# First modulation of a transformer kernel in eight pieces, and its first projection multiplied one feature tile at a time

## The reference

```python
c_act = jax.nn.silu(c)                               # (1, 1024)
mod = c_act @ ada_w[layer] + ada_b[layer]            # (1, 6 * 1024)
sh1, sc1, g1, sh2, sc2, g2 = jnp.split(mod, 6, -1)
hmix = rmsnorm(x, norm_mix[layer]) * (1.0 + sc1) + sh1
proj = hmix @ w_in                                   # hgrn2_mixer: q, f, v, g, 1024 columns each
q, f_pre, i_in, g = jnp.split(proj, 4, -1)
log_f = jnp.log(lb + (1.0 - lb) * jax.nn.sigmoid(f_pre))
k = (1.0 - lb) * jax.nn.sigmoid(-f_pre)
```

## Time and profile before

| | |
|---|---|
| median of 3 runs | 2296.42 us (2296.18 to 2296.62) |
| profiled execution, first to last instruction (span) | 2294.8 us |
| around the span (median less span; the page gives no other time of the profiled execution) | 1.6 us |
| PE busy | 98% of the span, granted clock 0.998 |
| DVE, ACT, POOL busy | 72%, 46%, 28% |
| first matmul of a projection | 39.7 us after the span's start |

### The profile page before, as it was taken

How to read it: one execution, slowest core, us unless ns; L and a number is a source line. 1 busy time by engine, 2 the same in 40 slices (tenths; PEclk the granted TensorE clock), 3 DMA queues, 4 the chain that set the end, 5 groups by cost and what they waited for, 6 DMA issues and landing times.

```text
span 2294.8 us, 34769 instructions
## 1 busy us (share of the span) xinstructions
PE 2247.6 (98%) x14151; PEld 1950.4 (85%) x14151; DVE 1641.8 (72%) x2121; ACT 1051.0 (46%) x1515; POOL 634.8 (28%) x559
## 2 busy tenths in 40 slices
PE   7999999999999999999999999999999999999999
PEld 5888778999887877778999888999887868899987
DVE  6668557889785456637888657989456984788844
ACT  4322534555334457734555346444345363544432
POOL 0110223332122048803332011332011870233200
PEclk9999999999999999999999999999999999999999
DMA  8654156775763210026774526775333202787322
GB/s 333 191 166 140 46 174 165 185 180 122 267 211 102 82 57 1 1 65 168 190 185 119 162 95 173 175 185 120 101 97 98 81 30 76 191 191 173 105 92 83
DMA packets 224373, 308.69 MB, mean 135 GB/s; under 512 B 14345, under 2 KB 165446, under 8 KB 223958
## 3 DMA queue, kind: packets, MB, share of 16 engines
q1 hardware_dynamic: 173268, 223.99, 30.1%
q0 software_dynamic: 50640, 82.29, 17.4%
q10 hardware_dynamic: 306, 0.19, 0.0%
HBM read 302.23 MB, written 4.19 MB: 134 GB/s over the span
## 4 chain that ended last, share of the span: by engine, by line
PE 85%; DVE 9%; POOL 2%; ACT 2%; issue 1%; DMA 1%; ACTq 0%; DVEq 0%
PE ps L733 42%; PE ps L1181 10%; PE ps L1183 10%; PE ps L1182 10%; PE ps L880 4%; DVE w_lo L2320 2%; DVE dsa_mask L3127 1%; PE ps L1307 1%; POOL nsa_p L3498 1%; PE ps L1323 1%; DVE small L3125 1%; PE ps L929 1%; ACT w_hi L1635 1%; DMA m_raw<-in_ada_w 1%; DVE h_lo L2417 1%
## 5 line engine op out<-in xcount | busy, mean ns | idle before, releaser
L2320 DVE TENSOR_TENSOR w_lo<-w_raw,w_hi 128x1024 fp32r<-128x1024 f32 (+1 forms) x466 | 652.5, 1401 | 478.7 <-ACT w_hi L1635 477.0
L1635 ACT ACTIVATE w_hi<-w_raw 128x1024 fp32r<-128x1024 f32 (+1 forms) x472 | 495.7, 1051 | 996.0 <-PE ps L733 577.6
L1181 PE MATMUL ps<-feat_t,w_hi 128*128 128x256 f32 x1152 | 326.5, 283 | 3.1 <-DVE hid L2824 2.3
L1182 PE MATMUL ps<-feat_t,w_hi 128*128 128x256 f32 x1152 | 326.0, 283 | 0.0
L1183 PE MATMUL ps<-feat_t,w_lo 128*128 128x256 f32 x1152 | 326.0, 283 | 0.0
L3351 POOL TENSOR_TENSOR w_raw<-w_raw,w_raw 128x1024 f32<-128x1024 f32 x72 | 177.7, 2468 | 456.8 <-DVE w_lo L2320 456.8
L733 PE MATMUL ps<-h_hi,w_hi 128*128 128x512 f32 (+1 forms) x712 | 279.7, 393 | 3.8 <-DVE w_lo L2320 2.2
L733 PE MATMUL ps<-h_lo,w_hi 128*128 128x512 f32 (+1 forms) x712 | 277.2, 389 | 0.0
L733 PE MATMUL ps<-h_hi,w_lo 128*128 128x512 f32 (+1 forms) x712 | 277.2, 389 | 0.0
L1181 PE MATMUL ps<-h_hi,w_hi 128*128 128x256 f32 x864 | 244.9, 283 | 1.9 <-DVE w_lo L2320 1.9
L1182 PE MATMUL ps<-h_lo,w_hi 128*128 128x256 f32 x864 | 244.5, 283 | 0.0
(11 more groups left out here) (464 smaller groups left out, 4219.2 us busy)
## 6 DMA issues: line engine op xcount, KB each, us to landing
w_raw<-in_ffn_w_up SPq DMA_DIRECT2D x126, 512.0 KB, 6.5
w_raw<-in_ffn_w_down SPq DMA_DIRECT2D x176, 256.0 KB, 3.3
w_raw<-in_ffn_w_up POOLq DMA_DIRECT2D x72, 512.0 KB, 7.6
m_raw<-in_ada_w POOLq DMA_DIRECT2D x56, 512.0 KB, 4.7
w_raw<-in_ffn_w_gate SPq DMA_DIRECT2D x54, 512.0 KB, 5.9
w_raw<-in_hg_w_in SPq DMA_DIRECT2D x64, 256.0 KB, 3.1
w_raw<-in_ffn_w_up SPq DMA_DIRECT2D x48, 256.0 KB, 3.1
w_raw<-in_nsa_w_in SPq DMA_DIRECT2D x40, 256.0 KB, 2.9
```

Source lines behind the costliest of these rows:

```text
L1181: K.nc.tensor.matmul(out, hi[:, w], m_hi, start=opens and kt == f == 0, stop=False, skip_group_check=True)
L1182: K.nc.tensor.matmul(out, hi[:, w], m_lo, start=False, stop=False, skip_group_check=True)
L1635: K.nc.scalar.activation(K.half(K.hi(u), width), K.half(K.raw(u), width), ACT.Copy) \
L2320: K.nc.vector.tensor_tensor(K.half(K.lo(u), width), K.half(K.raw(u), width), hi, ALU.subtract) \
```

## The change

1. **Modulation by pieces.** sh1 and sc1 are made in eight pieces, one for each tile of 128 features. Piece kt is a load of 1024 rows x 128 columns for the shift and one for the scale (rows of 512 bytes), three buffers. DVE adds it up in eight instructions of 128x256, PE sums with two one-column matmuls, DVE adds the bias and makes the scale, 128x2 and 128x1.
2. **Norm.** The squares are summed by token on x as loaded (two 128x1024 tiles by ACT, two by DVE); the factor is spread over partitions by four matmuls on a diagonal. POOL multiplies x by it (`x_normed`, 128x512); ACT makes `h_hi` and the unrounded `h_whole` from it; DVE subtracts.
3. **f tile by tile.** A unit of f is one feature tile by 896 columns (7 PSUM banks); the last 128 columns of all eight tiles are a ninth unit. POOL makes `w_lo` of the first eight (128x896). The 192 f matmuls stay 192.
4. **Mod units.** None beside f; two beside each q unit, loaded four ahead. The decays move from load 12 to load 7.
5. The rows of small vectors are loaded by ACT's queue, all of them, ahead of its first work; silu(c) is made of Exp and a reciprocal, so one table of functions serves the head.

```diff
-FIRST = 5
+FIRST = 3
+FIRST_TILES = 7
...
+        self.unit["hg", "f"] = len(self.units)
+        for kt in range(KD):
+            one([(None, slice(0, wide), w[kt * P:(kt + 1) * P, D:D + wide])], wide)
+        one([(slice(0, KD), slice(0, P), w[:, D + wide:2 * D].rearrange("(k p) c -> p k c", p=P))])
...
-        nc.sync.dma_start(K.first[u % FIRST], K.io["ada_w"][0, u % KD * P:(u % KD + 1) * P, u // KD * D:(u // KD + 1) * D]) \
+    for kt in range(KD):
+        if kt >= FIRST:
+            sp.wait_ge(*K["mod_ready"].at(("first", kt - FIRST, KD - 1)))
+        for part in range(2):
+            c0 = part * D + kt * P
+            nc.sync.dma_start(K.first[kt % FIRST][:, :, part, :], K.io["ada_w"][0, :, c0:c0 + P].rearrange("(r p) c -> p r c", p=P)) \
+                .then_inc(*K.first_landed[kt % FIRST].more(kt))
+        weights(kt)
...
+def tensor_first_mod(K, kt):
+    K.pe.wait_ge(*K["mod_ready"].at(("first", kt, KD - 1)))
...
+        ins = K.nc.tensor.matmul(K.ps[:, 7, at:at + 1], K.first_acc[:, kt % 2, part * P:(part + 1) * P], K.ones[:, 0:1], start=True, stop=True)
...
+def tensor_hgrn_first(K):
+    for kt in range(KD):
...
+                mm(K.ps[:, n, :], hi[:, cols[n]], K.h_hi[:, kt, :], start=kt == 0, stop=False)
+            pe.wait_ge(*w_low(K, u))
+            for n in range(FIRST_TILES):
+                mm(K.ps[:, n, :], lo[:, cols[n]], K.h_hi[:, kt, :], start=False, stop=False)
+            tensor_first_mod(K, kt + 1)
+            pe.wait_ge(*K["h_low"].at(("hg_in", kt)))
+            for n in range(FIRST_TILES):
+                ins = mm(K.ps[:, n, :], hi[:, cols[n]], K.h_lo[:, kt, :], start=False, stop=False)
...
+    def weighted(kt):
+        acc = K.first_acc[:, kt % 2, :]
...
+        for r in range(KD):
+            raw, cr = K.first[kt % FIRST][:, r, :, :].rearrange("p a c -> p (a c)"), K.cvec[:, r:r + 1]
...
+                dve.wait_ge(*K["mod_ready"].at(("first", kt, r - 1)))
+                ins = nc.vector.scalar_tensor_tensor(acc, raw, cr, acc, ALU.mult, ALU.add)
...
+    for kt in range(KD):
+        if kt + 1 < KD:
+            weighted(kt + 1)
+        low(kt)
+        if kt + 1 < KD:
+            shift_and_scale(kt + 1)
...
+        for _ in range(2):
+            vector_mod_unit(K, m)
+            m += 1
...
+def gpsimd_first(K):
+    def normed(kt):
...
+        nc.gpsimd.tensor_tensor(K.x_normed[:, kt, :], K.xT[:, kt, :], K.rstd_spread[:, :], ALU.mult).then_inc(*K["pool_step"].up(("x_normed", kt)))
+    def low(u):
+        pool.wait_ge(*K["w_high"].at(u))
...
+        nc.gpsimd.tensor_tensor(K.half(K.lo(u), width), K.half(K.raw(u), width), hi, ALU.subtract).then_inc(*K["w_low_pool"].up(u))
+    normed(0)
+    for kt in range(KD):
+        low(u0 + kt)
+        if kt + 1 < KD:
+            normed(kt + 1)
```

More of the change, by code:

```diff
@@ L663, in tensor_start @@
-    tensor_norm_rest(K, "first", 0)
-    pe.wait_ge(*K["vec_copied"].at(3))
-    for part in range(2):
-        pe.wait_ge(*K["mod_ready"].at(("first", 8 * part + 7)))
-        tensor_mod_columns(K, (0, part), part, 4 + part)
-        tensor_stay_busy(K, 12 if part == 0 else 5, 7)
+    pe.wait_ge(*K["x_in"].at(0))
+    turn_x(7)
+    pe.wait_ge(*K["x_in"].at(1))
+    pe.wait_ge(*K["small_vec"].at("token_diagonal"))
+    for t in range(TT):
+        ins = nc.tensor.matmul(K.ps[:, 1, t * P:(t + 1) * P], K.ones, K.diagonal[:, t, :], start=True, stop=True)
@@ new lines, in scalar_start @@
+    act.wait_ge(*K.x_landed.at("all"))
+    ss = K.token_factor
+    for t in range(2):
+        nc.scalar.activation(K.squares[t][:, :], K.xin[:, t, :], ACT.Square, accum_out=ss[:, t:t + 1]).then_inc(*K["squared"].up(("first", t)))
+    act.wait_ge(*K["squared"].at(("first", 1)))
+    act.wait_ge(*K["squares_by_vector"].at(("first", 3)))
+    nc.scalar.activation(ss, ss, ACT.Ln, bias=K.eps, scale=1.0 / D).then_inc(*K["rstd"].up(("first", "ln")))
+    act.wait_ge(*K["rstd"].at(("first", "ln")))
@@ L1654, in scalar_start @@
+    for kt in range(3):
+        keep(kt)
+    act.wait_ge(*K["x_squares_summed"].at("factors_spread"))
+    nc.scalar.activation(K.rstd_spread[:, :], K.ps[:, 1, :], ACT.Copy).then_inc(*K["rstd"].up("first"))
+    scalar_split(K, 0)
+    for kt in range(3, 6):
+        keep(kt)
+    features(0)
+    keep(6)
     e = K.small[:, 48:64]
-    act.wait_ge(*K["small_vec"].at("lb_less"))
     nc.scalar.activation(e, e, ACT.Exp).then_inc(*K["small_act"].up("lb"))
-    scalar_split(K, 0)
-    scalar_norm_apply(K, "first", "hg_in", lambda kt: K.mod[:, 0, 0, kt:kt + 1], "ms01")
+    scalar_split(K, 1)
@@ L1661, in scalar_squares @@
+    for kt in range(1, KD):
+        features(kt)
+        scalar_split(K, kt + 1)
 def scalar_squares(K, tag, first, last):
@@ new lines, in low @@
+    def low(kt):
+        dve.wait_ge(*K["h_high"].at(("whole", kt)))
+        nc.vector.tensor_tensor(K.h_lo[:, kt, :], K.h_whole[kt % 2][:, :], K.h_hi[:, kt, :].bitcast(F32), ALU.subtract) \
+            .then_inc(*K["h_low"].up(("hg_in", kt)))
+    weighted(0)
+    for tile in range(1, len(K.vec_rows)):
+        keep_rows(tile)
+    dve.wait_ge(*K["x_turned"].at(KD - 1))
+    nc.vector.tensor_copy(K.xT[:, KD - 1, :], K.ps[:, first_bank(KD - 1), :]).then_inc(*K["vec_copied"].up("x_in"))
+    dve.wait_ge(*K["vec_copied"].at(1))
```

328 lines of the change are left out of this document (195 added, 133 removed).

## The result

| | before | after |
|---|---|---|
| median | 2296.62 us (7 runs, with those shown before) | 2303.89 us (7 runs) |
| ratio after / before | | 1.0029, 95% interval 1.002 to 1.0039 |
| span of the profiled execution | 2294.8 us | 2303.0 us |
| first q product, that is the end of f | 83.6 us | 88.5 us |

What follows compares the result with a forecast made beforehand. PE, busy 98% of the span, was taken as the bound, so the end of f decides: 9.8 (f) + 1.0 (clock) + 0.3 (q units) = +11.1 us, 2307.5 us; range 2298 to 2319, its own 2301 to 2316.

Steps and rivals of the forecast that it cites:

- The sign and its cause: Slower: in the head, POOL stops DVE's steps with two SBUF tensors, so f ends 9.8 us later.
- the wait for oneself: DVE's small steps in the head: each waits 0.105 us for the one before, so a piece takes 4.6 us.
- The hold: DVE stopped by POOL in the head: 2.55 us per period, 17.3 in all, plus 3.4 ahead of tile 0's scale.
- The clock: PE at half clock after idle stretches in the head, mainly in the last tile: +1.0 us, bounds 0 and 3.
- The q units: Second mod step and POOL's decays beside the q units nearly fit into DVE's idle time: +0.3 us, bounds 0 and 3.
- Transfers: Loads of the head's pieces at 195 to 260 GB/s: 5.2 to 6.5 us with weights, hidden in the 8.15 us period.
- rival 3: Transfers bound the head's pieces: 12 us each with weights, f ends near 118, +34 us, 2330; chance 0.05.
- Rival 4: PE at half clock through the head becomes the bound: f ends near 110, +26 us, 2322; chance 0.07.
- Rival 2: Head steps a tenth shorter, half of POOL's work falls where DVE waits: f ends at 79 to 88, within 0.2%; chance 0.08.
- Rival 1: POOL hardly holds DVE's small steps in the head: f ends at 72.8 to 78, 5 to 10 us faster; chance 0.10.
- The 4.3 us: Estimate from the skill's page: with no part of a DVE step hidden, f would end 4.3 us later than summed.
- From 140 us on nothing should change but the start: Behind the head, from 140 us to the end, the kernel only starts later and is otherwise unchanged.

## Why the prediction was right, and where it was off

**The sign and its cause were right.** f's end moves because DVE's small steps stand still while POOL computes: 18.9 us lost, 20.7 forecast; POOL's share of it is shown by taking the hold away (783 to 490 ns), by doubling a part of POOL's work and by giving another part to DVE. A step with one operand in PSUM loses nothing at all (490 ns beside 485 alone). It also works the other way: POOL's x_normed took 1419 ns in the mean, 1286 alone, and 1649 where it met h_lo. The Trainium skill (SBUF — State Buffer, "SBUF: two separate sides") says that whichever of the two starts first has the pair for its whole instruction; the trace agrees, with x_normed at 39.66 running until 41.41 behind the h_lo that was in its way.

**The step that failed in size is the wait for oneself.** "So 7 x (0.485 + 0.105) + 0.45 = 4.6 us": I took 0.105 us from steps four times as wide; on 128x256 it is 0.036, and a free piece takes 4.0. Over 56 steps that is 4 us, most of the 5.4 by which the scale of tile 7 came earlier than forecast (75.6, not 81.0). The hold was 1.8 us smaller too, but DVE's waits for PE's sums, 2.7 us in all and 1.8 of them behind the products at half clock, gave about as much back. From there the rest was as worked out, 12.9 us to the end of f against 12.1.

With 0.036, about 0.23 of the 0.52 us that a short step takes would not depend on its width (an estimate from 1.28 + 0.105 at four times the width), so "most of a short step is fixed" is too much.

**The clock** was priced at +1.0; 0.15 us are shown, from the first scale to the sixth. **The q units** were +0.3; 0.5 were measured (the distance is 4.96 us at their start and 5.42 at the first product behind them, 127.09 before and 132.51 now), as the decays held DVE's w_lo, one of them for 3.92 us. **Transfers** were hidden as said, and rival 3 fell with them, but packets of 512 bytes were faster than the forecast's 195 to 260 GB/s: at 14 to 20 us, where 3325 of 3468 packets were under 2 KB, the queues moved 363 GB/s. Rival 4 failed too, PE's half clock did not last.

**Rival 2, no change, came closer than its 0.08.** Its two conditions held in good part: a step with its wait was 12% shorter than forecast (0.521 for 0.590 us), and 36% of POOL's work cost DVE nothing. It had f's end at 79 to 88 us; 88.5 was measured.

**Some terms do not add up as written.** Rival 1's 72.8 should be 60.3 + 12.1 = 72.4. The 4.3 us by which a lock with nothing hidden would move the end can't be rebuilt: what the sum itself hides of DVE's steps is seven times 0.26 and 1.3 ahead of tile 0, about 3. The 3.6 us in rival 3 are set against 5.4 for a piece without its weights, and the text doesn't say which of the two they mean. The end of f before is 83.58, not the reckoned 83.3. None of these moves the forecast by more than 0.3 us.

**"From 140 us on nothing should change but the start" was wrong**, by 1.6 us and the clock's share. The ninth unit of f changes the turn of every later buffer. It was in the change's own first lines; I had counted its products and not its buffer. So 11.1 us against the 8.2 between the profiled executions are a head that was 5.8 us too dear (10.8 against 5.0) and a tail of some 2.7 that was missing, 1.6 of it from the buffers. That the two errors have opposite signs is luck: without the tail the time would have come near 2301 us, at the lower end of the forecast's own range (2301 to 2316).

## What to carry to other kernels

Before giving elementwise work to POOL beside short DVE steps, look at DVE's operands: with two SBUF tensors they stop for as long as POOL runs on SBUF tensors, down to a 128x1 step, and with one in PSUM they do not. An accumulator in PSUM moved the end of f by 9.4 us, giving POOL's larger half back to DVE by 5.4. Measure a step's own wait at its own width. When an edit is to keep the clock up, look at the windows of the whole stretch: a half-clock stretch may only have moved. And when a change adds one unit to a ring of buffers, list which unit holds each buffer at every place where the ring changes size.
